# A chunked recurrence on one Trainium2 core: all four 64x64 tiles of TensorE, and each chunk's tail overlapped with the next chunk's levels

## What is computed

```python
def step(S, inp):
    r_t, d_t, k_t, v_t, kk_t, akk_t = inp
    s_kk = jnp.einsum('bhvk,bhk->bhv', S, kk_t)
    S = S * d_t[:, :, None, :] - s_kk[..., None] * akk_t[:, :, None, :] + v_t[..., None] * k_t[:, :, None, :]
    return S, jnp.einsum('bhvk,bhk->bhv', S, r_t)

S0 = jnp.zeros((B, N_HEADS, HEAD_DIM, HEAD_DIM), F32)
_, o = lax.scan(step, S0, (tm(r_h), tm(decay), tm(k_h), tm(v_h), tm(kk), tm(kk * a_h)))
```

## Time and profile before

| what | value |
|---|---|
| median of 3 runs | 2303.47 us (2300.72 to 2304.05) |
| the profiled execution's own time | 2305.91 us |
| its span, first to last instruction | 2304.1 us |
| granted TensorE clock, mean over the span | 0.957 |
| TensorE busy | 1995.7 us, 87% |
| VectorE, ScalarE, POOL busy | 855.4, 402.7, 192.9 us |
| the recurrence, 230 to 465 us | 235 us, TensorE busy 224.9 |

### The profile page before, as it was taken

One profiled execution on the slowest core, in us unless ns is written; L12 is line 12 of the kernel. 1 busy time (PEld: TensorE's weight loads), 2 busy tenths in 40 slices (PEclk: granted clock), 3 DMA queues, 4 the chain that ended last, 5 costly groups with the idle time before them and its releaser, 6 DMA issues.

```text
span 2304.1 us, 34022 instructions
## 1 busy us (share of the span) xinstructions
PE 1995.7 (87%) x14412; PEld 1106.9 (48%) x14412; DVE 855.4 (37%) x1608; ACT 402.7 (17%) x975; POOL 192.9 (8%) x234
## 2 busy tenths in 40 slices
PE   6999999899998888788775999999998888777773
PEld 5843999874855322222222445546855322222221
DVE  6655655493465111000003474751565110100003
ACT  1052333220122000000002003611112010000001
POOL 1000212020000111111110000000000111111110
PEclk9999999999998999899998999999998999999997
DMA  4310000223344999999996222023344999999995
GB/s 148 109 38 3 10 4 5 93 74 110 98 195 188 365 404 401 406 409 405 404 409 256 70 76 74 1 84 118 112 183 190 385 401 406 409 406 408 400 410 203
DMA packets 115941, 510.95 MB, mean 222 GB/s; under 512 B 21552, under 2 KB 22712, under 8 KB 99424
## 3 DMA queue, kind: packets, MB, share of 16 engines
q1 hardware_dynamic: 104688, 492.15, 54.9%
q0 software_dynamic: 10880, 16.81, 2.2%
q10 hardware_dynamic: 240, 0.07, 0.0%
HBM read 503.73 MB, written 24.12 MB: 229 GB/s over the span
## 4 chain that ended last, share of the span: by engine, by line
PE 63%; DMA 20%; DVE 9%; SPq 4%; ACT 2%; issue 2%; ACTq 0%; POOLq 0%; DVEq 0%
DMA big<-in_moe_w 19%; PE ps L2455 12%; PE ps L1991 12%; PE ps L2116 9%; PE ps L1987 9%; PE ps L2484 4%; SPq L518 4%; PE ps L1970 2%; PE ps L2068 2%; PE ps L2256 1%; PE ps L2354 1%; PE ps L2366 1%; PE ps L1957 1%; PE ps L2262 1%; PE ps L2283 1%
## 5 line engine op out<-in xcount | busy, mean ns | idle before, releaser
L2455 PE MATMUL ps<-big 128*64 128x512 f32 x2048 | 473.5, 616 | 66.6 <-DMA big<-in_moe_w 63.4
L2455 PEld LDWEIGHTS ps<-big 128*64 128x64 f32 x2048 | 160.5, 141 | 330.2 <-issue 318.7
L1991 PE MATMUL ps<-big 128*128 128x512 f32 x672 | 289.9, 592 | 0.2 <-DVE big L1203 0.2
L2484 PE MATMUL ps<-big 128*64 128x512 f32 x1024 | 254.1, 642 | 32.5 <-ACT big L1122 32.5
L1845 DVE SCALAR_TENSOR_TENSOR big<-big,ps 128x256 f32<-128x256 f32 x64 | 26.9, 421 | 520.8 <-ACT big L1115 520.8
L2116 PE MATMUL ps<-big 64*64 64x64 f32 (+1 forms) x6144 | 207.8, 225 | 12.1 <-issue 6.8
L2116 PEld LDWEIGHTS ps<-big 64*64 64x64 f32 x6144 | 202.0, 137 | 15.5 <-issue 7.0
L1991 PEld LDWEIGHTS ps<-big 128*128 128x128 f32 x672 | 127.3, 190 | 159.5 <-issue 158.5
L1987 PE MATMUL ps<-big 128*128 128x256 f32 x896 | 196.8, 383 | 6.3 <-DVE big L1345 6.3
L1987 PEld LDWEIGHTS ps<-big 128*128 128x128 f32 x896 | 172.0, 192 | 30.3 <-issue 6.5
L1836 DVE TENSOR_TENSOR big<-ps,gain_ffn 128x512 f32<-128x512 f32 x66 | 45.6, 691 | 356.3 <-PE ps L2490 356.3
(11 more groups left out here) (339 smaller groups left out, 2040.5 us busy)
## 6 DMA issues: line engine op xcount, KB each, us to landing
big<-in_moe_w SPq DMA_DIRECT2D x182, 2048.0 KB, 33.3
big<-in_rw_wrkv SPq DMA_DIRECT2D x12, 1024.0 KB, 5.2
big<-in_mx_wkv SPq DMA_DIRECT2D x12, 1024.0 KB, 5.0
big<-in_moe_w SPq DMA_DIRECT2D x12, 1024.0 KB, 27.7
big<-in_mb_wqkv SPq DMA_DIRECT2D x12, 1024.0 KB, 6.4
big<-in_mx_wq SPq DMA_DIRECT2D x8, 1024.0 KB, 6.3
big<-in_mx_wo SPq DMA_DIRECT2D x8, 1024.0 KB, 5.1
big<-in_moe_w SPq DMA_DIRECT2D x16, 512.0 KB
```

The lines of the kernel that those rows point to most:

```text
L1991: ins = mm(d[:], lhsT=acts[:, k, i * P:(i + 1) * P], rhs=quarter(w)[:, k], start=k == 0, stop=k == 3)
L2455: ins = mm(ps[2 + b][half * BR:(half + 1) * BR, :], lhsT=hgT[b][:, k], rhs=w13[set_][:, :, k, half * 256:(half + 1) * 256], start=k == 0, ...
L2484: ins = mm(ps[5 + b][half * BR:(half + 1) * BR, :], lhsT=hT[b][:, c0:c0 + BR], rhs=w2[set_][:, f, half * HB:(half + 1) * HB], start=f == 0 ...
```

## The change

Three things change in the recurrence.

1. **Tiles.** Some products are written into the other half of the partitions ("across"), on the tiles rows 0-63 by columns 64-127 and rows 64-127 by columns 0-63, while the products beside them stay in their own half. `both_ways` alternates a crossed and a straight product: X (across) with Y (own) in levels 0 to 3, the turned X (across) with the gram of kappa (own). `ahead_b` mixes the gram of beta (own) with the turned beta and kappa (across); `out_and_state` mixes the output (across) with the state (own). The crossed and the straight product go to different banks. Since a crossed result has the two heads swapped, ScalarE copies it out in two halves of 64 partitions (`crossed`). T products, level 4's Y, right side and solve stay on two tiles.
2. **Order.** Right side, solve, output and state of chunk c-1 now stand between the levels of chunk c, and the preparing products of chunk c+1 behind levels 3 and 4. The loop runs to `CH + 1`. On VectorE `prepare` of chunk c+1 stands around level 1, one group before it and one behind.
3. **Buffers and counts.** Y of odd levels has a buffer of its own (`Yo`), and the step counts differ by group.

The number of matmuls in the program stays: 3456. The diff, cut to its core:

```diff
-def chunk_steps():
+def chunk_steps(g):
...
+    for c in range(CH + 1):
+        behind, ahead = (lambda *steps: of(c - 1, *steps)), (lambda *steps: of(c + 1, *steps))
+        pe += of(c, "xy1") + behind("rhs") + of(c, "xy2", "t2") + behind("u") + of(c, "xy3", "t3") + behind("s", "o")
+        pe += of(c, "xy4", "t4") + ahead("gram_b", "turned") + of(c, "y5", "t5") + ahead("y0", "gram_k") + of(c, "t6")
...
+            def crossed(dst, src, scale=1.0):
+                for h in range(2):
+                    to, at = slice(h * L, (h + 1) * L), slice((1 - h) * L, (2 - h) * L)
+                    ins = A(dst[to], src[at], ACT.Copy, scale=scale)
+                return ins
...
-                        A(groups[g]["X"][c % 2], half_bank(g, 1), ACT.Copy).then_inc(act_done[g], 1)
+                crossed(groups[g]["X"][c % 2], half_bank(g, 1)).then_inc(act_done[g], 1)
...
+            for c in range(CH + 1):
+                if c < CH:
                     for g in range(2):
-                        level(g, c, i)
-                    if i < 2 and c + 1 < CH:
+                        level(g, c, 0)
+                    for i in range(1, 3):
+                        if c + 1 < CH:
+                            prepare(i - 1, c + 1)
                         for g in range(2):
-                            (masked_b, masked_k)[i](g, c + 1)
-                if c + 2 < CH:
+                            level(g, c, i)
+                if c:
                     for g in range(2):
-                        prepare(g, c + 2)
...
+                        state_on(g, c - 1)
...
+            def both_ways(across, own):
+                (dst_a, lhs_a, rhs_a, width_a), (dst_o, lhs_o, rhs_o, width_o) = across, own
+                for q in range(GP):
+                    for h in range(2):
+                        r, other = slice(h * L, (h + 1) * L), slice((1 - h) * L, (2 - h) * L)
+                        a = mm(dst_a[other, q * width_a:(q + 1) * width_a], lhsT=lhs_a[r, q], rhs=rhs_a(r, q), start=True,
+                               stop=True)
+                        o = mm(dst_o[r, q * width_o:(q + 1) * width_o], lhsT=lhs_o[r, q], rhs=rhs_o(r, q), start=True,
+                               stop=True)
+                return a, o
...
                 if i < 4:
-                    each_head(bank4[1], L, (Y, of(X))).then_inc(pe_done[g], 1)
-                if i < 5:
-                    each_head(bank4[2], L, (X, of(Y))).then_inc(pe_done[g], 1)
-                if i:
-                    each_head(bank4[3], L, (Y, of(Tm))).then_inc(pe_done[g], 1)
...
+                    both_ways((bank4[1], Y, of(X), L), (bank4[2], X, of(Y), L))[1].then_inc(pe_done[g], 1)
+                else:
+                    each_head(bank4[1], L, (X, of(Y))).then_inc(pe_done[g], 1)
...
+            def out_and_state(g, c):
...
+                    for i, (lhs, rhs) in enumerate(((rho, of(b["S"])), (K, v), (Bn, of(b["u"])))):
+                        for h in range(2):
+                            r, other = slice(h * L, (h + 1) * L), slice((1 - h) * L, (2 - h) * L)
+                            o = mm(out_[other, cols], lhsT=lhs[r, q], rhs=rhs(r, q), start=i == 0, stop=i == 2)
+                            if i < 2:
+                                lhs_s, rhs_s = ((kt, v), (bt, of(b["u"])))[i]
+                                s = mm(state[r, cols], lhsT=lhs_s[r, q], rhs=rhs_s(r, q), start=i == 0, stop=i == 1)
```

More of the change, by code:

```diff
@@ L939, in y0_out, with kappa_out @@
+            def kappa_out(g, c):
+                wait_pe(act, g, c, "turned")
+                crossed(groups[g]["kt"][c % 2], half_bank(g, 3, 1)).then_inc(act_done[g], 1)
             def y0_out(g, c):
                 wait_pe(act, g, c, "y0")
-                A(groups[g]["Y"][c % 2], half_bank(g, 0), ACT.Copy).then_inc(act_done[g], 1)
-            for c in range(2):
-                for g in range(2):
-                    exponentials(g, c)
+                crossed(groups[g]["Y"][c % 2], half_bank(g, 1, 1)).then_inc(act_done[g], 1)
@@ L946, in _, with out_out @@
+            def out_out(g, c):
+                wait_pe(act, g, c, "o")
+                crossed(chunk_of(r_all, g, c), half_bank(g, 3)).then_inc(act_done[g], 1)
             for g in range(2):
-                turned_out(g, 0)
+                exponentials(g, 0)
+            for g in range(2):
+                beta_out(g, 0)
+                kappa_out(g, 0)
             for g in range(2):
                 y0_out(g, 0)
-            for c in range(CH):
-                for i in range(4):
+            for c in range(CH + 1):
+                if c < CH:
@@ L1465, in prepare @@
                 if c:
-                    wait_pe(dve, g, c - 1, "turned")
+                    wait_pe(dve, g, c - 1, "gram_k")
                 V.tensor_tensor(b["beta"], ak, b["gro"], ALU.mult).then_inc(dve_done[g], 1)
@@ new lines, in _, with ahead_b @@
+            upper = slice(GP * L, 2 * GP * L)
+            halves = [(slice(h * L, (h + 1) * L), slice((1 - h) * L, (2 - h) * L)) for h in range(2)]
+            def ahead_b(g, c):
+                b = groups[g]
+                beta, ar = b["beta"], b["ar"][c % 3]
+                wait_dve(pe, g, c, "kappa")
+                if c >= 2:
+                    wait_act(pe, g, c - 2, "o")
+                    wait_dve(pe, g, c - 2, "s_add")
+                for q in range(GP):
+                    for r, other in halves:
+                        gram = mm(ps[4 * g][r, q * P:(q + 1) * P], lhsT=beta[r, q], rhs=ar[r, q], start=True, stop=True)
+                    m = beta if q < 2 else b["kappa"]
+                    for p in range(2 * (q % 2), 2 * (q % 2) + 2):
+                        cols = slice((q // 2 * GP + p) * L, (q // 2 * GP + p + 1) * L)
+                        for r, other in halves:
+                            t = mm(ps[4 * g + 3][other, cols], lhsT=m[r, p], rhs=ident[r, r], start=True, stop=True)
+                gram.then_inc(pe_done[g], 1)
+                t.then_inc(pe_done[g], 1)
@@ new lines, in ahead_k, with square @@
+            def ahead_k(g, c):
+                b = groups[g]
+                wait_dve(pe, g, c, "bn")
+                if c:
+                    wait_act(pe, g, c - 1, "y5")
+                y0, gram = both_ways((ps[4 * g + 1][:, upper], b["X"][c % 2], turn, L),
+                                     (ps[4 * g], b["kappa"], of(b["ar"][c % 3]), P))
+                y0.then_inc(pe_done[g], 1)
+                gram.then_inc(pe_done[g], 1)
+            def square(g, c, i):
+                bank4, X, Y = ps[4 * g:4 * g + 4], groups[g]["X"][c % 2], y_of(g, c, i)
```

289 lines of the change are left out of this document (169 added, 120 removed).

## The result

| what | before | after |
|---|---|---|
| median | 2303.47 us (2300.72 to 2306.99, 5 runs) | **2283.88 us** (2282.63 to 2291.26, 5 runs) |
| profiled execution, its span | 2305.91, 2304.1 us | 2291.26, 2289.5 us |
| mean granted TensorE clock | 0.957 | 0.954 |
| start of the group norm (end of the stage) | 466.01 us | 448.54 us |

The ratio is 0.9932, interval 0.9913 to 0.9952: 19.6 us faster, where 59 were forecast. 2244 was a quarter of the way into the range of 2232 to 2284, and the time landed at its far end, near the 2286 where the price of instruction fetch at its upper bound had put it.

What follows compares the result with a forecast made beforehand. TensorE was taken to bound the recurrence. Start 238.0 plus 16.8 + 117.3 + 22.6 + 8 + 4 = 168.7 ends it at 406.7 instead of 466.0; 2303.5 - 59.3 = 2244 us, range 2232 to 2284.

Steps and rivals of the forecast that it cites:

- the price of instruction fetch at its upper bound: TensorE's instruction blocks at 3.6 us each, 6.9 per chunk: a chunk of 24.8 us and a total of 2286.
- Four tiles run together at 58 ns: TensorE in the recurrence: a round filling all four 64x64 tiles takes 58 ns, against 117 ns if they do not overlap.
- ScalarE's copies of the two outputs: Sign in a middle chunk: output-and-state copies of the two groups come 1.4 us apart instead of 2.33.
- Rivals 2 and 3: Tiles sharing rows or columns take turns: straight pairs still pair, 2298; or no neighbours overlap, 2415, slower. Chance 0.09 each.
- The other engines: Work per chunk of the recurrence: VectorE 15.9 us as before, ScalarE 13.5 us with copies split in halves.
- The wait for T6: At each chunk's start TensorE's level 0 waits for VectorE's T6 of group 1, about 0.6 us.
- Rival 4: VectorE, at 83% of the chunk, becomes the bound; one more us per chunk, 2252; chance 0.65 together with the main case.
- Instruction fetch: TensorE's instruction blocks: 1.1 to 3.6 us each, taken near the low end, adding 0.4 us to the 19.15 us period.
- The loads and the memory norm: Beside and after chunk 6: 8 us lost to fetch stops under 5 MB of loads, 4 us to the norm.
- Rival 1: Pace of issue or fetch holds the four tiles back: 22 ns per record gives 2267, 26 ns gives 2283; chance 0.17.
- The ends: Start and finish of the recurrence: level 0 begins 2.7 us earlier, at 238.0; chunk 7 with its tail takes 22.6.
- The gain passes through: After the recurrence: what follows moves with its end, so the 59 us saved there shorten the whole run.

Runs made afterwards that it cites:

- after_again: The changed kernel run again with no edit, for a second profile; 2279.27 us, ratio 0.9908 to the kernel before.
- e2_merged: The changed kernel with X and T side by side, one 128-column product replacing two of 64 in levels 1 to 3; 2265.36 us, ratio 0.9853.
- e6_waits_after: The changed kernel with 250 already met waits per chunk added to TensorE's stream behind the squarings of X and Y; 2485.46 us, ratio 1.0809.
- e7_waits_before: The kernel before the change with the same 250 already met waits per chunk added to TensorE's stream; 2514.71 us, ratio 1.0929.

## Why the prediction was wrong in size

**Four tiles run together at 58 ns: right.** The 32 records of a call start within 0.47 us, as said. The outputs and states of the two groups follow each other at 1.40 us instead of 2.33 where no stop falls between them. VectorE's timeline has the state updates behind them:

```profile
345.32 0.42 DVE L1543 TENSOR_TENSOR big<-ps,big 128x256 f32<-128x256 f32 x1 [2.07 <-PE ps L2280]
345.77 0.42 DVE L1545 TENSOR_TENSOR big<-big 128x256 f32<-128x256 f32 x1
346.72 0.42 DVE L1543 TENSOR_TENSOR big<-ps,big 128x256 f32<-128x256 f32 x1 [0.52 <-PE ps L2280]
```

Four of the eight chunks in after have 1.40; in the others a stop makes it 2.6 to 3.2. ScalarE's copies of the two outputs, the sign that was forecast, begin 2.85 us apart in this same chunk (345.42 and 348.27), since the stop that ends at 347.97 lies between. Rivals 2 and 3 (tiles that take turns, 2298 and 2415) are out. Of the Trainium skill, page "TensorE: Matmul & The Clock Gate", neither rule that the prediction weighed holds here: weight loads of 129 to 135 ns (L2187) overlap matmuls of the same rows, with four records in every 58 ns (section on packing small matmuls), and the mean distance between starts is 58 / 4 = 14.5 ns, not at least 25 (section "Wait — 56ns, not 53.3ns?").

**The other engines: right, or near.** VectorE's 15.9 us per chunk came to 15.08, ScalarE's 13.5 to 15.47: 16 half copies at the pace of L944 (1.56 us for 4) cost more than I had for them. Neither is on the path. The wait for T6 was put at 0.6 us per chunk. In the list of waits, 240 to 390 us, it is

```profile
PE ps L2187 <- DVE big L1538: 4.1, 8, 1.4
```

L1538 is the addition to T of every level. Two of the 8 waits lie inside chunk 0, behind VectorE's prepares (1.42 and 0.55 us); the six at the start of a chunk, which are the wait for T6, are 0.25 to 0.39 us each. Rival 4 did not come.

**Instruction fetch: the step that failed.** "To this I add 0.4 for instruction fetch ... so I stay near the low end." The bounds were 1.1 and 3.6 us per block; the runs show 3.7 to 3.8 on the mean, a little past the upper one. The transfer of 1.0 us, which the low end took for the cost, is only its middle part: a packet starts about 1.3 us after TensorE has gone on with the block before it, and TensorE goes on again about 1.4 us after the packet has ended. This one term carries most of the miss: the five middle periods are 25.23 us in after_again and 25.85 in after, forecast 19.55. Over the stage of after_again, chunks counted from their first level copy, which comes 1.15 us after level 0 starts (so chunk 7's 22.6 is 21.5 here, and level 0 at 238.0 a copy at 239.2):

| part | forecast | after_again | too low by |
|---|---|---|---|
| first level copy of chunk 0, at | 239.2 | 238.0 | -1.2 |
| chunk 0 | 16.8 | 18.6 | 1.8 |
| chunks 1 to 5 | 97.75 | 126.2 | 28.4 |
| chunk 6 with loads and memory norm | 31.55 | 35.3 | 3.8 |
| chunk 7 and tail | 21.5 | 24.7 | 3.2 |

36 us in all; 2244 + 36 = 2280, measured 2279.27. The loads and the memory norm were put at 12 us in chunk 6. Its excess over a middle chunk is 10.1 (35.3 less 25.2), so this allowance was about right, and the line's 3.8 is the middle chunk's own miss less 2. The argument against the upper end was that stops had come only under load. That shows only that a block without load takes no longer than TensorE then needed for one. It left out that nothing in the whole recurrence used blocks faster, so no row spoke for a smaller value; the stops under load had the packet later, and I took their absence elsewhere for slack. The kernel before used a block every 4.05 us and the service takes 3.7: it ran a tenth away from this limit, with no wait to show it. The range has a slip too: no cost of fetch (0.4 for six chunks) and 5 us instead of 8 for the loads take 5.4 us off 2244, which gives 2239 and not 2232.

**Rival 1 named this outcome** (2267, and 2283 at 26 ns), by a smoother mechanism: a pace per record that stretches each round. Full rounds run at 58 ns and the loss comes in stops. Its signs, "stops named issue of 1 us and more outside the loads", were the ones found. It had a chance of 0.17, too little for a limit that no row excluded.

**The ends.** The first level copy moved from 241.9 to 237.33 in after and 238.03 in after_again, 4.6 and 3.9 us where 2.7 were forecast. The loads: the stops of 3.65 and 3.90 us in chunk 6 are as forecast, a block that comes later while 5 MB come in. **The gain passes through: right.** In after_again the stage ends 23.2 us earlier and the span is 23.6 shorter (2280.5 for 2304.1), in e2_merged 39.9 and 41.0; in the profile of after 17.5 and 14.6, the least close of the three.

Left open: what fills the 1.3 us before a packet and the 1.4 us behind it; what makes the whole 3.69 in one run and 3.79 in another; and a filler with no cost of its own, which would have shown the stops without touching the arithmetic. Sharing one moving operand between two products (alpha and rho with S, K and k with v) would take more instructions out; it wasn't tried.

## What to carry to other kernels

Before packing small matmuls tighter, count TensorE's instructions per us: each f32 matmul here is four (two records, two weight loads), and the stream came at 256 per 3.7 us, 69 per us, whatever the tiles could do. A resource that just keeps up leaves no wait in the profile, so the pace at which it is used now is the only pace that is shown, and anything faster is to be priced at that bound. Where the limit was reached, wider matmuls that do two products with one lhsT still paid: 14 us here, with hardly less work on the array.

## What the runs showed of the hardware

- Four 64x64 tiles with f32 operands run at four records per 58 ns at a granted clock of 1.00, those that share rows or columns included (after, 336.58 to 336.64).
- TensorE's instructions come in packets of 16 KB with 256 instructions, waits counted, one per 3.7 to 3.8 us on the mean where TensorE keeps stopping for them. A packet starts about 1.3 us after matmuls have gone on, takes 1.0 us, and they go on again about 1.4 us after its end. With 5 MB of loads in flight a packet started 3.6 us after, and a stop grew from 1.45 to 3.65 us.
- An instruction that only waits for what is already met costs TensorE up to about 0.1 us (e6_waits_after, e7_waits_before), the lower clock included.
